# Rounded input and its remainder as one 512-column matmul into a pair of PSUM banks

## The reference

```
def swiglu(h, w_in, w_out):
    gate, up = jnp.split(h @ w_in, 2, axis=-1)
    return (jax.nn.silu(gate) * up) @ w_out

x = x + 0.5 * swiglu(rmsnorm(x, ffn1_norm[layer]), ffn1_w_in[layer], ffn1_w_out[layer])
...
```

## Time and profile before

| | |
|---|---|
| time, median of 3 runs | 2947.69 us (2946.51 to 2948.51) |
| the profiled execution's own time, its span | 2946.25 us, 2944.4 us |
| busy: TensorE matmul, weight load | 2735.7 us (93%), 2639.0 us (90%) |
| busy: VectorE, ScalarE | 1861.1 us (63%), 1411.1 us (48%) |
| mean granted TensorE clock | 0.965 of full speed |

### The profile page before, as it was taken

One profiled execution on the slowest core, in us unless ns is written; L12 is line 12 of the kernel. 1 busy time (PEld: TensorE's weight loads), 2 busy tenths in 40 slices (PEclk: granted clock), 3 DMA queues, 4 the chain that ended last, 5 costly groups with the idle time before them and its releaser, 6 DMA issues. The chain is left out here.

```text
span 2944.4 us, 49086 instructions
## 1 busy us (share of the span) xinstructions
PE 2735.7 (93%) x21094; PEld 2639.0 (90%) x21094; DVE 1861.1 (63%) x2387; ACT 1411.1 (48%) x1896; POOL 0.2 (0%) x4
## 2 busy tenths in 40 slices
PE   7998989999987898999998998789998899999998
PEld 7998889999987788999898997679987899989998
DVE  5657656656666645666646847968455476665764
ACT  5444545454474354545455446254453445445443
POOL 0000000000000000000000000000000000000000
PEclk9999999999998999999999998989998899999999
DMA  6553535555533133555534553135532255443463
GB/s 207 181 189 121 168 115 197 187 184 189 186 137 97 61 129 108 195 188 170 183 117 149 185 192 121 43 117 181 195 129 78 91 191 189 171 164 122 158 200 130
DMA packets 129001, 450.11 MB, mean 153 GB/s; under 512 B 20112, under 2 KB 20368, under 8 KB 128528
## 3 DMA queue, kind: packets, MB, share of 16 engines
q1 hardware_dynamic: 128784, 446.97, 45.1%
HBM read 445.47 MB, written 1.44 MB: 152 GB/s over the span
## 5 line engine op out<-in xcount | busy, mean ns | idle before, releaser
L248 PE MATMUL B<-R,WH 128*128 128x256 f32 x10432 | 2092.2, 284 | 85.5 <-DVE R L912 39.2
L248 PEld LDWEIGHTS B<-R,WH 128*128 128x128 f32 x10432 | 1688.3, 191 | 101.9 <-DVE R L912 29.7
L846 DVE TENSOR_TENSOR WL<-SL,WH 128x1024 fp32r<-128x1024 f32 x836 | 1010.4, 1223 | 766.0 <-ACT WH L1772 764.8
L248 PE MATMUL B<-R,WL 128*128 128x256 f32 x4480 | 1263.9, 282 | 0.0
L1772 ACT ACTIVATE WH<-SL 128x1024 fp32r<-128x1024 f32 x836 | 865.5, 1052 | 541.6 <-PE B L248 437.8
L248 PEld LDWEIGHTS B<-R,WL 128*128 128x128 f32 x4480 | 857.8, 191 | 0.0
L248 PE MATMUL B<-RB,WH 128*128 128x256 f32 x1984 | 556.4, 280 | 0.2 <-DVE WL L846 0.2
L248 PE MATMUL B<-RB,WL 128*128 128x256 f32 x1728 | 482.0, 279 | 0.0
L248 PEld LDWEIGHTS B<-RB,WH 128*128 128x128 f32 x1984 | 374.3, 189 | 0.6 <-DVE WL L846 0.4
L248 PEld LDWEIGHTS B<-RB,WL 128*128 128x128 f32 x1728 | 324.8, 188 | 0.0
L248 PE MATMUL B<-WH,R 128*128 128x512 f32 x480 | 159.1, 406 | 2.9 <-DVE WL L846 2.9
(11 more groups left out here) (281 smaller groups left out, 1561.9 us busy)
## 6 DMA issues: line engine op xcount, KB each, us to landing
SL<-in_w SPq DMA_DIRECT2D x836, 512.0 KB, 3.8
CP<-in_cp SPq DMA_DIRECT2D x5, 768.0 KB, 6.0
X<-in_xT SPq DMA_DIRECT2D x2, 512.0 KB, 6.6
PG<-in_mem SPq DMA_DIRECT2D x1, 1024.0 KB, 10.7
out<-X SPq DMA_DIRECT2D x1, 1024.0 KB, 3.9
PK<-in_pk SPq DMA_DIRECT2D x1, 598.5 KB, 3.8
dn_y<-PG SPq DMA_DIRECT2D x1, 256.0 KB, 2.2
PG<-dn_y SPq DMA_DIRECT2D x16, 16.0 KB, 1.8
```

The costliest lines, as they stand in the source:

```text
L248: return p.matmul(o, left, right, start=first, stop=final, skip_group_check=True)
L846: v.tensor_tensor(WL[t % NSPL][:, :], SL[t % NRAW][:, :], WH[t % NSPL][:, :].bitcast(F32), ALU.subtract).then_inc(s_lo, 1)
```

## The change

Of 3104 blocks of the kind above, 2560 become "paired". In a paired block the rounded activation and its remainder are one 512-column moving operand (`both`, two runs of 256 columns of one common buffer): per half, one matmul of `WH` with 512 columns fills a whole bank (columns 0 to 255 the rounded part, 256 to 511 the remainder's part), and one of `WL` with 256 columns is added to the first part. A half takes two matmuls where it took three, and a group fills two banks where it filled one, so that the four banks hold two groups. The remaining 544 blocks (the first groups of stages that begin late or interleave, and the stages in `ALONE`) stay as they were. The 512-column stages are not touched.

Because the sum now lies in two parts, a paired group is taken in two steps. ScalarE copies the remainder's part of both banks to the destination in SBUF (`leftover`, L1940 of the changed kernel, 178 instructions of 128 x 512), and VectorE adds the first part to it (`summed`, L1002, or `completed`, L1062) before its instruction of before. Where a group is added to x, VectorE does both parts itself, in two dependent instructions (L1035, L1037). In `to_post` ScalarE now squares what VectorE has completed in Y8, and its copy to Y8 is gone. In `swiglu` and `mlp` the taking of a paired group moves from the end of its last block to the third block of the next group (`due_later`). In `mlp` VectorE's second instruction becomes `max(sum, 0) * inverse root`, and ScalarE squares it (L2398) before it rounds it (L2400).

The core of the diff:

```
+    def place_groups(self, banks):
+        self.first, self.needs, self.leaves = [], [], []
+        for j in range(self.groups):
+            mine = banks.take(1 if self.alone(j) else 2)
+            self.first.append(mine[0])
+            self.needs.append(sorted({banks.last[b] for b in mine if banks.last[b]}))
...
+LATE = ("f1.1.in", "f2.0.in", "f2.1.in", "ab.q", "xq0", "xq1")
+ALONE = ("dn.k", "dn.z", "dn.q", "dn.v", "c.in")
...
+        single = groups if name in ALONE else outer + 1 if outer else 2 if name in LATE else 0
...
                 for half in range(2):
-                    o, ws = bk[:, cc(half)], slice(at + half * 128, at + half * 128 + 128)
-                    mm(o, hi[:, ws], xh, k == 0 and half == 0, False)
-                    mm(o, hi[:, ws], xl, False, False)
+                    ws = slice(at + half * 128, at + half * 128 + 128)
+                    if st.alone(j):
...
+                    else:
+                        o = BK[st.bank(j, half)][:, 0:256]
+                        mm(r3(BK[st.bank(j, half)][:, :]), hi[:, ws], both, k == 0, False)
                     t = mm(o, lo[:, ws], xh, False, k == st.kc - 1)
...
+            def summed(name, j, d):
+                x, y, free = done(name, j)
+                if y is None:
+                    return x, free
+                v.wait_ge(rest.sem, rest[name, j])
+                v.tensor_tensor(d, x, d, ALU.add).then_inc(V.sem, V.up())
+                v.wait_ge(V.sem, V.n)
+                return d, free
...
-                    v.scalar_tensor_tensor(X[:, hc(j)], bk[:, :], scale, X[:, hc(j)], ALU.mult, ALU.add).then_inc(free, 1)
+                    x, y, free = done(name, j)
+                    d = r3(X[:, hc(j)])
+                    if y is not None:
+                        v.scalar_tensor_tensor(d, y, scale, d, ALU.mult, ALU.add).then_inc(V.sem, V.up())
+                        v.wait_ge(V.sem, V.n)
+                    v.scalar_tensor_tensor(d, x, scale, d, ALU.mult, ALU.add).then_inc(free, 1)
...
+            def completed(name, j, d):
+                x, _, free = done(name, j)
+                v.wait_ge(rest.sem, rest[name, j])
+                v.tensor_tensor(d, x, d, ALU.add).then_inc(free, 1)
...
-                        bk, free = done(name, x)
-                        v.tensor_tensor(r3(d), r3(bk[:, :]), RB2, ALU.mult).then_inc(free, 1)
-                        evacuated(name, x)
-                        v.scalar_tensor_tensor(d, d, 0.0, d, ALU.max, ALU.mult).then_inc(hid.sem, hid.give((f, x)))
...
+                    of, free = summed(name, x, r3(d))
+                    v.scalar_tensor_tensor(r3(d), of, 0.0, RB2, ALU.max, ALU.mult).then_inc(free, 1)
...
+            def leftover(name, j):
+                st = ST[name]
+                a.wait_ge(s_block, st.done(j))
+                y = PS[:, st.bank(j) * 512:st.bank(j) * 512 + 1024].rearrange("p (h a t) -> p h a t", a=2, t=256)[:, :, 1, :]
...
+                    t = a.activation(d, y, ACT.Copy)
+                t.then_inc(rest.sem, rest.give((name, j)))
...
-                    if j < 3 and bias is None:
-                        a.activation(SQ[:, hc(j)], bk[:, :], ACT.Square).then_inc(sq.sem, sq.give((n, j)))
...
+                    evacuated(name, j)
+                    if j < 3:
+                        square(n, j, Y8[:, hc(j)])
+                        continue
+                    for x, part in enumerate(("3a", "3b")):
+                        a.activation(SQ[:, cc(6 + x)], Y8[:, cc(6 + x)], ACT.Square).then_inc(sq.sem, sq.give((n, part)))
```

More of the change, by code:

```diff
@@ L41, in done, with alone, paired, released @@
         return self.at(j, self.kc - 1) + self.width
-    def bank(self, j, i=0):
-        return (self.turn + j * self.width + i) % 4
-    def used(self, j, i=0):
-        return (self.turn + j * self.width + i) // 4
+    def place_groups(self, banks):
[4 more added lines that the diff above has]
+            self.needs.append(sorted({banks.last[b] for b in mine if banks.last[b]}))
+            self.leaves.append([banks.leave(mine[i:i + 1] if self.width == 2 else mine) for i in range(self.width)])
+    def alone(self, j):
+        return self.width == 1 and j < self.single
+    def paired(self, j):
+        return self.width == 1 and j >= self.single
+    def bank(self, j, i=0):
+        return self.first[j] + i
+    def released(self, j, i=0):
+        return self.leaves[j][i]
+class Banks:
+    def __init__(self):
+        self.turn, self.last, self.count = 0, [None] * 4, [0] * 4
+    def take(self, n):
+        self.turn += self.turn % n
+        b = self.turn % 4
+        self.turn += n
+        return list(range(b, b + n))
+    def leave(self, mine):
+        self.count[mine[0]] += 1
+        for b in mine:
+            self.last[b] = (mine[0], self.count[mine[0]])
+        return self.last[mine[0]]
+LATE = ("f1.1.in", "f2.0.in", "f2.1.in", "ab.q", "xq0", "xq1")
+ALONE = ("dn.k", "dn.z", "dn.q", "dn.v", "c.in")
 def stage_table():
@@ L244, in build_program, with rest_to @@
         g_p = Signal(sem("s_g_p"), [0, 1])
+        def rest_to(name, j):
+            kind, jj = name.split(".")[-1] if "." in name else name[:2], slice(j * 512, j * 512 + 512)
+            if name in ("ab.o", "dn.o") or kind in ("out", "xo"):
+                return None
+            if kind == "in":
+                u = j // 2
+                return r3(PG[10][:, u % 4 * 512:u % 4 * 512 + 512] if j % 2 else Y8[:, u % 2 * 512:u % 2 * 512 + 512])
+            if kind == "up":
+                return r3(PG[10][:, j % 4 * 512:j % 4 * 512 + 512])
+            if kind in ("dn", "o"):
+                return r3(Y8[:, jj])
+            if name == "ab.x":
+                return PG[10][:, 0:1036].rearrange("p (c t) -> p c t", t=259)[:, 2 * j:2 * j + 2, 3:259]
+            if name == "g.r":
+                return r3(BIG[:, jj])
+            if kind[0] == "g" and name[0] == "r":
+                at = 4096 + int(kind[1]) * 1024 + j * 512
+                return r3(BIG[:, at:at + 512])
+            base, at = {"ab.k": (PG[2], 1024), "ab.g": (PG[3], 1024), "xk1b": (PG[0], 1024)}.get(name, (None, 0))
+            if base is None:
+                base = PG[1] if kind == "k" else PG[0] if kind == "xk" else PG[2]
+            return r3(base[:, at + j * 512:at + j * 512 + 512])
+        rest = Signal(sem("s_rest"), [(name, j) for name, st in ST.items() for j in range(st.groups)
+                                      if st.paired(j) and rest_to(name, j) is not None])
         def tensor_program(p):
+            AT03, AT45, AT67 = (0, 8192), (16384, 18432), (20480, 22528)
             def mm(o, left, right, first=True, final=True):
@@ L399, in attn_lru @@
                         t.then_inc(s_small, 1)
-                for j, k in gemm("xk0", R45, R45, 0, 2048):
+                for j, k in gemm("xk0", *AT45):
                     if j == 0 and k % 2 == 0:
@@ L438, in cross @@
                 through(normed(f"xq{layer}", n))
+                for name in ("xk0",) if layer == 0 else ("xk1a", "xk1b"):
+                    for j in range(ST[name].groups):
+                        evacuated(name, j)
                 for j in range(4):
@@ L837, in due, with due_later @@
             return (0, 1) if late and j == 1 else (j,)
+        def due_later(name, j, k):
+            st = ST[name]
+            if k == 2 and st.paired(j - 1):
+                return (j - 1,)
+            return tuple(x for x in due(name, j, k, True) if st.alone(x))
         def gains(name, base=0):
@@ L1780, in walk @@
                         hi(b // 4 + 3)
+                    if k == st.kc - 1 and st.paired(j) and rest_to(name, j) is not None:
+                        leftover(name, j)
                     yield j, k
@@ L1876, in tok_to, with to_post @@
                         a.activation(d, bk[:, :], ACT.Copy).then_inc(free, 1)
[L1878 to L1882 removed]
+            def to_post(name, n):
                 for j, k in walk(name):
@@ L2368, in conformer @@
                 logs()
-                for j, k in to_post("c.o", 14, gains("cbo")):
+                for j, k in to_post("c.o", 14):
                     pass
```

265 lines of the change are left out of this document (149 added, 116 removed).

## The result

| | before | after |
|---|---|---|
| time, median | 2947.80 us (4 runs, 2946.51 to 2948.51) | 2985.89 us (4 runs, 2981.05 to 2987.10) |
| ratio, 95% interval | | 1.0127 (1.0109 to 1.0144) |
| the profiled execution: time, span | 2946.25 us, 2944.4 us | 2985.81 us, 2984.0 us |
| mean granted TensorE clock | 0.965 | 0.955 |

What follows compares the result with a forecast made beforehand. TensorE's streaming was taken to bound long stages, serial chains over other engines the stage boundaries. Added chains of 21.9 us less 4 gave +18 us on 2946.25, 2964.2; forecast 2966 us as median, range 2943 to 2986.

Steps and rivals of the forecast that it cites:

- The pairs: In paired blocks, merging two 256-column matmuls into one of 512 saves 0 to 12 us, taken as 4 us.
- Groups added to x: At ends of stages added to x, one more dependent VectorE instruction: 5 x 0.73 = 3.7 us, plus 0.7 after f2.1.out.
- The cover that I counted on: In ab.q and f1.1.in TensorE doesn't wait for the sum, so nothing was added; 1.5 us if that cover were gone.
- to_post stages: At eight stage ends the last group's squares wait for copy and addition: 8 x 1.36 = 10.9 us.
- I put nothing: Granted clock after longer waits: costed at nothing; 1 us at each of some ten waits only for the upper end, 2980.
- Elsewhere: First mixer projections, g.r, xk0 and xk1: TensorE or weight tiles found later than VectorE, so 1 us allowed in all.
- Cross attention and retention: Copy and addition before the scores, 2 x 1.36 = 2.7 us; two additions before each retention output, 2.9 us for two blocks.
- Bank pairs come late: Rival: bank pairs freed after the 5.6 us group, thin place mlp with 0.20 us spare; 24 us more, 2990 us, chance 0.09.
- The two other rivals: Column rate belongs to the instruction, 2919 us, chance 0.14; copy and addition chains covered by existing waits, 2947 us, chance 0.14.
- the first rival: In paired blocks each pair saves 10 ns, 51 us in all, 2919 us; decides from 4.3 ns a pair; chance 0.14.
- The square on ScalarE: In mlp the square moves from VectorE to ScalarE, which is idle half the time; costed at nothing.
- The signs: 512-column matmuls 233 to 235 ns apart, m1.dn sums 1.4 us later, xq0 waiting 1.5, scores 2.4, no swiglu bank waits.

Runs made afterwards that it cites:

- e1: The changed kernel with no block paired, only the other edits kept; 2943.28 us, ratio 1.0011 to the kernel before.
- e2: The changed kernel with all four groups of ab.o, dn.o, xo0 and xo1 unpaired; 2974.17 us, ratio 1.0110 to the kernel before.
- e3: The changed kernel with only the last group of ab.o, dn.o, xo0 and xo1 unpaired; 2982.78 us, ratio 1.0135 to the kernel before.
- e4: The changed kernel with only the last group of r0.o, r3.o, c.o, g.o and m0.dn to m3.dn unpaired; 2973.81 us, ratio 1.0113.
- e10: The changed kernel with every group of m0.up to m3.up unpaired; 2982.13 us, ratio 1.0140 to the kernel before.
- e5: The changed kernel plus unread matmuls on TensorE at nine normalised stage ends, four ahead of the sums of squares and six behind; 2989.20 us, ratio 1.0150.
- e9: The changed kernel itself measured once more, nothing altered, on another chip; 2989.28 us, ratio 1.0156 to the kernel before.
- e13: The kernel before plus six unread matmuls behind the sums of squares at nine normalised stage ends; 2941.79 us, ratio 0.9993.
- e6: The changed kernel with r0.k, r3.k, xk0, xk1a and xk1b unpaired in all groups; 2988.20 us, ratio 1.0157 to the kernel before.
- e16: Repeat of e6: the changed kernel with r0.k, r3.k, xk0, xk1a and xk1b unpaired; 2991.62 us, ratio 1.0175 to the kernel before.
- e7: The changed kernel with 1800 of 2560 paired blocks kept, in stages where no chain was thought to wait; 2943.31 us, ratio 1.0000 to the kernel before.
- e11: The changed kernel with only 1350 of 2560 paired blocks kept, fewer than in e7; 2938.91 us, ratio 0.9985 to the kernel before.
- e12: The changed kernel with only 1110 of 2560 paired blocks kept, in the longest stages whose taking has room; 2938.38 us, ratio 0.9989 to the kernel before.
- e14: e12 plus six unread matmuls behind the sums of squares at nine normalised stage ends; 2932.42 us, ratio 0.9974 to the kernel before.
- e15: The changed kernel with m0.up to m3.up unpaired, plus the unread matmuls of e5; 2972.91 us, ratio 1.0119 to the kernel before.

## Why the prediction was right in sign and half in size

The step that failed is the counting of the added instructions: each was costed once, at the end of a stage. The runs showed 43.6 us of added waits where the sum had 21.9. An instruction added where the round of VectorE and ScalarE is already longer than a group counts in every group (11.2 us of waits for 3.7), and what it delays, the weight tiles and the banks, is waited for in stages that the sum put at 1 us (7.2 us of waits, 11.3 us of time). The clock, put at nothing, fell too, at a price that stays open.

- **The pairs: "5120 pairs save 0 to 12 us ... I take 4 us".** Mis-sized. By the account above the span without waits and clock lost 20 us against the kernel before and 15 us against e1, which has no pairs (2661.9 us): 3 to 4 ns a pair. I had taken the 512 columns from rows 4, where a 512 follows a 512, at twice 116.7 ns; here, between two matmuls of 256, a half block takes 347 ns and not 350, so a merged pair does save some ns; whether they went with the instruction or with its weight load, no run tells. The Trainium skill, "TensorE: Matmul & The Clock Gate", section Back-to-back issue gap, has columns / 2.4 plus 2.5 ns for an isolated matmul, and says that in a stream with weight loads both operations set the spacing. The 12.8 us that I had estimated from it came nearer than my 4 us, though its estimated 109 ns for 256 columns is below what any row here shows (116.7 to 118).
- **"Groups added to x: ... 5 x 0.73 = 3.7 us".** By its waits this failed worst, and e2 and e3 show why. It measured 12.4 us with the clock, 11.2 us of waits. Where the groups are long (f1.1.out into dn.k, 15 us a group) the term was nearly right: 1.1 us of wait. Behind ab.o, dn.o, xo0 and xo1 VectorE's round of 6.01 us already exceeded the group's 5.6, and the 0.73 counted in every group: 2.1 to 2.8 us more of wait at each start behind them, and e2 took off 2.6 each. The trace had this round, its first row just before those of rows 7, and I didn't measure it; I checked the rounds only for swiglu and mlp. The cover that I counted on in ab.q and f1.1.in was gone as well: 0.7 us of wait in each, the 1.5 us that the prediction named for that case.
- **"to_post stages ... 8 x 1.36 = 10.9 us".** Right as a wait: 1.46 us at seven of the eight ends, 1.61 at c.o, and e4 gave back 14.6 us. As time, with r0.q and the end, it was 21.0 us for 11.6. Late bank pairs in the up stages are part of that (4.8 us by e10), slow sums a small part (2.6 us), and the rest goes with the lower clock in the first blocks, whose price e5 leaves open.
- **"I put nothing" on the clock.** Not borne out, but the size is not shown. Half clock outside waits rose by 31.7 us, by the account 16 us of time (in e9, 10 us). The upper end had 10 us for it. It can't be read as a price per place: where the clock was held up (e5, e13), the time stayed within the measurement.
- **"Elsewhere ... allow 1 us in all".** Wrong by about 10 us, 7.2 us of it waits (with ab.q's), and r0.v0 and r3.v0 besides, 3.0 us each in the first profile, which stand in the retention line. Of the 11.3 us, 2.5 are in e1 as well, which has no pairs, with 10 us more half clock. e6 and e16 took these waits away in place, but not the time of the whole. I had found "TensorE or the weight tiles later than VectorE" there, but VectorE makes the tiles' remainders too: what it does longer, the tiles pay for.
- **Cross attention and retention.** The scores wait 2.43 us where 2.4 was forecast; r0.o and r3.o, behind the attention outputs, are 1.1 us longer each where 1.46 was. The rest of the lines is clock and r0.v0, r3.v0.
- **"Bank pairs come late".** The thin place in mlp does bite, 2.8 us of waits in five and 4.8 us by e10. The mechanism was right, the price of the rival, 24 us, was not. In swiglu there is one such wait, 1.9 us in f1.0.in.
- **The two other rivals are out.** A block takes 0.693 us, not 0.68: a pair saves some ns, as the first rival has it, but not the 4.3 from which it would have decided. The chains were not covered.
- **The square on ScalarE, at nothing:** right as far as e1 shows.
- **The signs.** As named: the sums behind m1.dn 1.4 us later (1.46) and the scores' wait (2.43). Not as named: 229 ns and not 233 to 235 from a 512 to the next matmul, 2.01 us and not 1.5 in xq0, with 1.43 us ahead of it, and the wait for a bank in f1.0.in.

The errors were of both signs, by the account some +38 us of chains and clock against -16 us of pairs, and partly cancelled, the luck of the clock in g.o included. That the time fell inside the stated range is owed to this.

## What to carry to other kernels

Before an instruction is costed once at a stage's end, measure the round of its engine, from one group's taking to the next and with its waits for other engines, against the group: where the round is already longer, the instruction counts in every group, and also delays whatever else that engine makes, here the weight tiles. A faster stream only pays where the next engine in line isn't already what ends last; otherwise TensorE arrives sooner and waits. Change a kernel stage by stage where the taking has room, not everywhere. Even so the gain is small: e7, e11 and e12 can't be told from the kernel before, and only e14, with the unread matmuls besides, is 0.26% faster.

## What was not expected of the hardware

- Matmuls of 512 and 256 columns in turn start 229 and 118 ns apart, 347 together; 256 alone 116.7 or 117.8, 512 alone 233.3.
- The same program's time goes with the clock it is granted. The changed kernel (e9) ran 2993 to 2997 us at a mean clock of 0.950 to 0.952 and 2979 to 2980 us at 0.957 to 0.958; the kernel before, beside it, 2944 to 2953 at 0.961 to 0.963 and 2930 to 2941 at 0.966 to 0.968. Differences under some 10 us in one profiled execution say nothing until they are placed in a stage.
- A higher clock is not less time by itself: the unread matmuls raised it to 0.968 (e5) and 0.973 (e13) with no gain that can be told. Nor is a lower mean always more time: 0.949 in place of 1 in e15's profile left m1.dn at 89.2 us. How much of the 38 us would vanish if the clock were held up everywhere stays open.
